# Row of the mLSTM decays: sent to all partitions by four DMAs instead of by products with a selecting row

## The chip, the cores and the metric

One Trainium2 chip, one of its NeuronCores. The metric is the device time of one execution in microseconds (us). The kernel before takes 950.82 us (median of three runs, 950.45 to 951.0).

## What is computed

One inference step of a hybrid streaming encoder with two layers. Two streams go through it together: a prompt of 256 new frames (T columns 0 to 255) and 64 sampled frames of a running stream (columns 256 to 319), so T = 320. A layer projects the normalised input into four head groups (a: convolution and linear recurrence, b: latent attention, c: retention, d: mLSTM), joins their outputs in an output projection, and ends in a SwiGLU network. All numbers are fp32. The change touches group d alone. Its step in the reference is:

```python
bh  = cumsum(lfc); igh = igc
dm  = where(tril, bh[..., :, None] - bh[..., None, :] + igh[..., None, :], -inf)
m_t = maximum(bh + m, max(dm, -1))
sc  = einsum('bthd,bshd->bhts', qc, kc) * exp(dm - m_t[..., None])
```

The kernel splits the exponent of one head h into a part that depends on the query t alone, `r2[h, t] = bh[t] - m[t]`, and a part that depends on the key s alone, `r1[h, s] = ig[s] - bh[s]`. Scores are kept with the keys on the partitions and the queries along the row. So r1 is a number per partition, and r2 is a row that all 128 partitions need.

## The kernel before, in words

Each engine has its own instruction stream, written out by hand in the order in which it runs (TensorE from line 694, ScalarE from 1262, VectorE from 1560, GpSimd from 586, the queue of weight loads from 502). They are tied by semaphores alone. The products of TensorE write eight banks of PSUM; `layer_uses` (129) gives each result its banks in order, `claim` makes TensorE wait until the previous user of a bank has been read, and `fill` signals that a result is there.

Weights stream through a ring of five slots; a slot is loaded again when its last product is done. Layers run one after the other. Within a layer the order on TensorE is: the input projections (`feature`, line 743: 16 instructions of 128x320 for an output of 128 rows), then stage d, stage b (attention), stage c (retention), the output projection (1068), and the SwiGLU products (1111), which take over half of the time.

Stage d is four heads long. TensorE runs `d_scores(0)`, and then for each head h: one projection for stage c (for h = 3 the key transposes of stage b and half a projection), `d_scores(h+1)` ahead of need, and `head_out(h)`, the value products. `d_scores(h)` is the three score products (771 to 773) and, for the decays, one product of the 4x128 table `headrow` with the 4x320 tile `r2` (928), which puts row h of r2 on all partitions, in bank 4 or 5 (`dd0` to `dd3`). VectorE then runs `decay_arg(h)`: three additions of a mask (1806) that read this bank and write `dmx`. ScalarE takes three exponentials of it (1415 to 1417) with r1 as the bias. VectorE multiplies the scores (1853) and the values (1801, the helper `tails`) by the result, which releases `head_out(h)` (`need(pe, "w_d", ...)`; its first product is line 781). VectorE's order is `decay_arg(0)`, and then for each h the multiplications of h, `decay_arg(h+1)`, after h = 0 the keys of stage b (`key_rows`, 1843 to 1846), and `d_out(h-1)` (1821 to 1834).

The row r2 is made by VectorE (1753) in 4 partitions, one for each head; 1756 is the last of that group of instructions and signals `m_rows`, on which GpSimd waits before it sends out the states `p_mm` and `s_mm` (recorded at line 615, the helper `out`). TensorE's products of stage d come some 21 us later.

`arena` is a scratch tile of 128 x 10624 numbers; `pr`, the attention probabilities, lies in it from `bstart + 1280`, and is first written in stage b. `latents_loaded` counts the loads of the attention's latents (three DMAs in each layer, 16 counts each).

Of the kernel before, what the change touches and what calls it, by code (L numbers as in the profile page):

```python
# [68 lines left out]
def constants():  # L69

    parts, at, n = [], {}, 0

    def put(name, a):
        nonlocal n
        full = np.zeros((P, a.shape[1]), np.float32)
        full[:a.shape[0]] = a
        at[name] = (n, a.shape[1])
        parts.append(full)
        n += a.shape[1]

    i = np.arange(P)
    put("ident", np.eye(P))
    put("ones", np.ones((P, P)))
    put("headmean", (i[:, None] // HD == i[None, :] // HD) / HD)
    put("swap", (i[:, None] == (i[None, :] ^ 32)))

    pos = np.concatenate([np.arange(SEQ), PAST + np.arange(DEC), np.zeros(TP - T)]).astype(np.float32)
    inv = (np.float32(10000.0) ** (-np.arange(16, dtype=np.float32) / np.float32(16))).astype(np.float32)
    ang = (pos[:, None] * inv[None, :]).astype(np.float32).reshape(NT, P, 16).transpose(1, 0, 2)
    put("cos_t", np.concatenate([np.cos(ang), np.cos(ang)], 2).reshape(P, NT * 32))  # L90
    put("sin_t", np.sin(ang).reshape(P, NT * 16))
    row_head = lambda pair: 2 * pair + i // HD
    put("headrow", np.repeat(np.eye(H), P, 1))
    put("pairrow", np.concatenate([(row_head(p)[None, :] == np.arange(H)[:, None]) for p in range(2)], 1))
    put("early", (i[None, :] < 64) * (i[:, None] == 0))
    put("late", np.where(i[:, None] == 0, NEG, 0.0) * np.ones((1, 64)))
    diff = np.full((P, 512), -1, np.int64)
    diff[:, 0:256] = np.arange(256)[None, :] - i[:, None]
    diff[:, 256:384] = np.arange(128)[None, :] - i[:, None]
    diff[:, 448:512] = np.arange(64)[None, :] - i[:, None]  # L100
    ok = diff >= 0
    put("negmask", np.where(ok, 0.0, NEG))
    lg = np.log(1.0 - 2.0 ** (-5.0 - np.arange(H)))
    put("decay", np.concatenate([np.where(ok, np.exp(np.where(ok, diff, 0) * lg[h]), 0.0) for h in range(H)], 1))
    put("cross", np.concatenate([np.exp((np.arange(DEC)[None, :] + 1.0) * lg[row_head(p)][:, None])
                                 for p in range(2)], 1))
    inv = (np.float32(10000.0) ** (-np.arange(32, dtype=np.float32) / np.float32(32))).astype(np.float32)
    ang = (pos[None, :T] * inv[i % 32][:, None]).astype(np.float32)
    put("cos_f", np.cos(ang))
    put("sin_f", np.sin(ang) * np.where(i % 64 < 32, -1.0, 1.0)[:, None])  # L110
    return np.concatenate(parts, 1).astype(np.float32), at
# [17 lines left out]
def layer_uses():  # L129
    u = [("cpT", (2,)), ("ms1", (3,))]  # L130
    u += [(f"kv{i}", (i + 1,)) for i in range(3, KTILES)]
    dense = [0]

    def d(*names):
        for n in names:
            u.append((n, (dense[0] % 2,)))
            dense[0] += 1

    d("ql0", "ql1", "kvr", "mo0", "mo1", "mig", "mfg", "mv0", "mv1")
    u += [("cnT", (4,)), ("qms", (5,))]  # L140
    d("mvt0", "mvt1")
    u += [("qt0", (6,)), ("qt1", (7,)), ("qt2", (2,))]
    d("mq0", "mq1", "mk0", "mk1")
    u += [(f"kv{i}", (4 + i,)) for i in range(3)]
    u += [("rT", (3,)), ("gx", (2,)), ("mkt", (6, 7))]
    for h in range(H):
        u += [(f"ds{h}", (2 + h % 2,)), (f"dd{h}", (4 + h % 2,)), (f"do{h}", (6 + h % 2,))]
    d("rq0", "rq1", "rk0", "rk1")
    fill = [("rv1",), ("rqs0", "lx0", "rqs1", "rvt0", "rvt1"), ("rks0", "lx1", "rks1"), ("rg0",)]
    u += [("bk0", (4, 5)), ("bq0", (6,))]  # L150
    d("rv0")
    u += [("bs0", (2, 3))]
    for h in range(H):
        if h == 1:
            u += [("dT", (0, 1))]
        if h + 1 < H:
            u += [(f"bk{h + 1}", (4, 5)), (f"bq{h + 1}", (6,))]
        d(*fill[h])
        u += [(f"bp{h}", (4, 5))]
        if h + 1 < H:  # L160
            u += [(f"bs{h + 1}", (2, 3))]
        else:
            u += [("ga0", (6,)), ("gx0_", (2,)), ("ga1", (3,))]
            d("gx1_", "rg1")
        u += [(f"bo{h}", (7,))]
    u += [("rkt", (4, 5)), ("bT", (6, 7))]
    for h in range(H):
        u += [(f"cs{h}", (2 + h % 2,)), (f"co{h}", (4 + h % 2,))]
    d("lg0", "lg1")
    u += [("am0", (6,)), ("am1", (7,)), ("cT", (6, 7))]  # L170
    u += [(f"o{n}", (n,)) for n in range(KT)]
    u += [("ms2", (2,)), ("fa0", (0,)), ("fb0", (1,))]
    for j in range(1, FT):
        u += [(f"fa{j}", (3 * (j % 2),)), (f"fb{j}", (3 * (j % 2) + 1,)), (f"fc{j}", (3 * (j % 2) + 2,))]
    for q in range(NQ):
        u += [(f"ya{q}", (3 * (q % 2),)), (f"yb{q}", (3 * (q % 2) + 1,)), (f"yc{q}", (3 * (q % 2) + 2,))]
    return u
# [25 lines left out]
def build(nc, I, O):  # L203
    with ExitStack() as ctx:
# [5 lines left out]
        def sem(name):  # L210
            if name not in sems:
                sems[name] = ctx.enter_context(nc.semaphore(name))
            return sems[name]
# [6 lines left out]
        def C(name, rows=P):  # L220
            a, n = cat[name]
            return cst[0:rows, a:a + n]
# [31 lines left out]
        def view(base, n, **kw):  # L254
            assert base + n <= AR, (base, n)
            return arena[:, base:base + n]
# [29 lines left out]
        qT = view(bstart + 896, TP)  # L286
        pr = view(bstart + 1280, 1024)
        pT = view(bstart + 2304, 1024)

        b = 0  # L290
        xpad = take(2 * 326).rearrange("p (k n) -> p k n", k=2)
# [99 lines left out]
        def claim(pe, use, l):  # L391

            for prev in before[use]:
                if prev is not None:
                    k = banks[prev][0]
                    pe.wait_ge(read[k], l * nfill[k] + order[prev])
                elif l > 0:
                    for k in {banks[last[b_]][0] for b_ in banks[use]}:
                        pe.wait_ge(read[k], l * nfill[k])
                else:  # L400
                    top = max(banks[use])
                    pe.wait_ge(sem("x_turned"), top + 1)
                    if 0 in banks[use]:
                        pe.wait_ge(sem("cols_ready"), 1)

        def bank(use, a, n, rows_=P):
            base = banks[use][0] * 512
            return flat[0:rows_, base + a:base + a + n]
# [4 lines left out]
        def need(eng, name, l, n, k=None):  # L413

            assert per.setdefault(name, n) == n, name
            eng.wait_ge(sem(name), l * n + (n if k is None else k))
# [16 lines left out]
        def now_read(eng, use):  # L433

            eng.sem_inc(read[banks[use][0]], 1)
# [151 lines left out]
        def _(pool):  # L587
# [25 lines left out]
            def out(dst, src):  # L613
                nout[0] += 1
                pool.dma_start(dst, src, allow_slow_non_contiguous=True).then_inc(sem("out_done"), 16)  # L615
# [12 lines left out]
            for l in range(DEPTH):  # L628
# [22 lines left out]
                out(O["p_krope"][l, 0].rearrange("(t p) c -> p t c", p=P), krr[:, 0:2, :])  # L651
                out(O["s_krope"][l, 0], krr[0:DEC, 2, :])
                need(pool, "m_rows", l, 1)
                out(O["p_mm"][l].rearrange("b h -> h b"), mro[:, SEQ - 1:SEQ])
                out(O["s_mm"][l].rearrange("b h -> h b"), mro[:, T - 1:T])
                pool.wait_ge(sem("out_done"), 16 * nout[0])
# [38 lines left out]
        def _(pe):  # L695
            mm = nc.tensor.matmul

            def fill(ins, use):
                ins.then_inc(filled[banks[use][0]], 1)
# [104 lines left out]

            def past_latents(l):
                claim(pe, "cpT", l)
                pe.wait_ge(sem("latents_loaded"), 48 * (l + 1))
                for a in range(4):
                    ins = nc.tensor.transpose(bank("cpT", a * P, P), pckv[:, a, :], ident)
                fill(ins, "cpT")  # L810

            for l in range(DEPTH):
# [109 lines left out]

                def d_scores(h):
                    causal_scores(f"ds{h}", l, h)
                    u = f"dd{h}"
                    claim(pe, u, l)
                    sel = C("headrow", H)[:, h * P:(h + 1) * P]
                    fill(mm(bank(u, 0, T), sel, r2[:, :], start=True, stop=True), u)  # L928

                def turn_keys(h, what="kq"):  # L930
                    if "k" in what:
# [629 lines left out]
        def _(dve):  # L1561
# [92 lines left out]
            for l in range(DEPTH):  # L1654
# [146 lines left out]
                    return v.tensor_tensor(vw[:, h % 2, :, 0:e], vaug[:, :, h, 0:e], end, ALU.mult)  # L1801

                def decay_arg(h):
                    wait_filled(dve, f"dd{h}", l)
                    for a, q0, n in ((0, 0, 256), (256, 128, 128), (448, 256, 64)):
                        step(v.tensor_tensor(dmx[:, a:a + n], bank(f"dd{h}", q0, n), C("negmask")[:, a:a + n], ALU.add),
                             "dmx" if a == 448 else None)
                    now_read(dve, f"dd{h}")

                def d_out(h):  # L1810

# [375 lines left out]
```

## Time and profile before

| | |
|---|---|
| median of three runs | 950.82 us |
| the profiled execution, its own time | 950.9 us |
| its span, first to last instruction | 949.1 us |
| TensorE busy (PE) | 939.3 us, 99% |
| VectorE (DVE), ScalarE (ACT), GpSimd (POOL) busy | 505.5, 203.7, 394.6 us |
| TensorE's granted clock | 1.0 (2.4 GHz) |
| moved by DMA | 112.12 MB, 118 GB/s on average |

PE is the matrix engine's products, PEld its weight loads, SP the queue that issues weight loads. Times in the profile are us from the start of the span. An fp32 product shows as two MATMUL instructions. POOL's DMA_DIRECT2D rows are GpSimd issuing a DMA in software; their duration is the issue alone and not the transfer.

### The profile page before, as it was taken

Reading aid. Unit: us, or ns where it says so; the run is one execution under the profiler, and the core shown is the slowest. Engines: PE = TensorE matmul, PEld = TensorE weight load, DVE = VectorE, ACT = ScalarE, POOL = GpSimd, SP = SyncE. Lnnn points to the kernel's source line nnn. Section 1 sums busy time; section 2 is a strip of 40 time slices with the busy share of each in tenths; the row PEclk is TensorE's granted clock in tenths of the full one; section 3 lists DMA queues with packets and bytes.
Section 4 is the critical chain, followed back from the end, with each engine's and each line's share of the span. In section 5 each row is a group of like instructions: output and inputs, shape, how many; then the busy total and the mean of one; then the engine's idle time right before and its main releaser. Section 6 shows DMA issues by size and latency. Waiting matters only on the chain.

```text
span 949.1 us, 14973 instructions
## 1 busy us (share of the span) xinstructions
PE 939.3 (99%) x5782; PEld 822.1 (87%) x5782; DVE 505.5 (53%) x1037; ACT 203.7 (21%) x445; POOL 394.6 (42%) x385
## 2 busy tenths in 40 slices
PE   8999999999999999999999999999999999999998
PEld 6776777877999999999977677777789999999998
DVE  5473656864555656512253555668346565653321
ACT  2223244433011000100031243454320000001001
POOL 6200200033976666676311003002159666666770
PEclk9999999999999999999999999999999999999999
DMA  9942211308555444343443312121375444444421
GB/s 280 234 134 90 89 47 46 93 8 217 145 148 146 135 134 135 122 153 126 120 129 112 106 61 76 35 75 50 65 195 140 134 134 133 136 136 136 139 87 47
DMA packets 159314, 112.12 MB, mean 118 GB/s; under 512 B 10118, under 2 KB 157228, under 8 KB 159116
## 3 DMA queue, kind: packets, MB, share of 16 engines
q1 hardware_dynamic: 154660, 104.50, 37.9%
q0 software_dynamic: 3952, 5.92, 2.4%
q8 instruction: 46, 0.75, 0.3%
q10 hardware_dynamic: 632, 0.75, 0.3%
q14 instruction: 24, 0.20, 0.1%
HBM read 108.89 MB, written 2.27 MB: 117 GB/s over the span
## 4 chain that ended last, share of the span: by engine, by line
PE 96%; DVE 1%; ACT 1%; ACTq 0%; issue 0%; POOL 0%; DVEq 0%; POOLq 0%
PE ps L1111 51%; PE ps L743 19%; PE ps L1068 7%; PE ps L1129 2%; PE ps L852 1%; PE ps L824 1%; PE ps L953 1%; PE ps L889 1%; PE ps L1007 1%; PE ps L1016 1%; PE ps L771 1%; PE ps L791 1%; PE ps L928 1%; PE ps L936 1%; PE ps L1049 0%; PE ps L781 0%
## 5 line engine op out<-in xcount | busy, mean ns | idle before, releaser
L743 PE MATMUL ps<-hT,ring 128*128 128x320 f32 x672 | 187.9, 435 | 2.2 <-DVE hT L1580 1.7
L743 PEld LDWEIGHTS ps<-hT,ring 128*128 128x128 f32 x672 | 124.9, 190 | 56.2 <-DVE hT L1580 3.9
L604 POOL TENSOR_TENSOR work<-ring 128x512 f32<-128x512 f32 (+1 forms) x66 | 81.7, 1238 | 155.2 <-issue 112.6
L1111 PE MATMUL ps<-mixT,ring 128*128 128x160 f32 x672 | 105.0, 299 | 0.0
L1111 PE MATMUL ps<-hT,work 128*128 128x160 f32 x672 | 98.5, 299 | 0.0
L1111 PE MATMUL ps<-hT,ring 128*128 128x160 f32 x672 | 98.1, 299 | 0.0
L1111 PEld LDWEIGHTS ps<-mixT,ring 128*128 128x128 f32 x672 | 95.9, 190 | 0.0
L1111 PEld LDWEIGHTS ps<-hT,ring 128*128 128x128 f32 x672 | 93.7, 190 | 0.3
L1111 PEld LDWEIGHTS ps<-hT,work 128*128 128x128 f32 x672 | 93.7, 190 | 0.0
L606 POOL TENSOR_TENSOR work<-ring 128x512 f32<-128x512 f32 (+1 forms) x66 | 82.2, 1246 | 5.2
L605 POOL TENSOR_TENSOR ring<-ring 128x512 f32<-128x512 f32 (+1 forms) x66 | 82.2, 1245 | 5.2
L607 POOL TENSOR_TENSOR work<-ring,work 128x512 f32<-128x512 f32 (+1 forms) x66 | 81.9, 1241 | 5.2
L1532 ACT ACTIVATE arena<-ps 128x160 f32<-128x160 f32 x42 | 12.7, 303 | 286.9 <-PE ps L1111 286.9
L1068 PE MATMUL ps<-mixT,ring 128*128 128x320 f32 x256 | 71.1, 435 | 0.0
L2120 DVE TENSOR_TENSOR arena<-arena,ps 128x160 f32<-128x160 f32 x8 | 2.6, 321 | 118.6 <-ACT arena L1550 118.6
L1068 PEld LDWEIGHTS ps<-mixT,ring 128*128 128x128 f32 x256 | 48.0, 190 | 19.2
L615 POOL DMA_DIRECT2D out_p_ret<-sst x8 | 4.2, 525 | 141.1 <-DVE sst L1978 141.1
L1111 PE MATMUL ps<-work,ring 128*128 128x160 f32 x352 | 55.7, 299 | 0.0
L1111 PE MATMUL ps<-mixT,work 128*128 128x160 f32 x336 | 52.5, 299 | 0.0
L1111 PE MATMUL ps<-arena,work 128*128 128x160 f32 x352 | 51.7, 299 | 0.0
L1111 PEld LDWEIGHTS ps<-work,ring 128*128 128x128 f32 x352 | 50.4, 190 | 0.0
L1111 PEld LDWEIGHTS ps<-arena,work 128*128 128x128 f32 x352 | 49.1, 190 | 0.0
(394 smaller groups left out, 1386.2 us busy)
## 6 DMA issues: line engine op xcount, KB each, us to landing
ring<-in_w_gu SPq DMA_DIRECT2D x88, 512.0 KB, 5.2
ring<-in_w_in SPq DMA_DIRECT2D x44, 512.0 KB, 4.8
ring<-in_w_down SPq DMA_DIRECT2D x32, 512.0 KB, 4.4
ring<-in_w_out SPq DMA_DIRECT2D x16, 512.0 KB, 4.4
ring<-in_w_down SPq DMA_DIRECT2D x16, 384.0 KB, 3.5
cst<-in_consts POOLq DMA_DIRECT2D x1, 1664.0 KB, 12.7
ring<-in_w_in SPq DMA_DIRECT2D x2, 640.0 KB, 5.3
wqb<-in_mla_wq_b POOLq DMA_DIRECT2D x2, 384.0 KB, 6.7
```

Of the source, the lines that this page charges most:

```text
L604: step(tt(s3, a11, a21, ALU.subtract))
L605: step(tt(a21, a21, a22, ALU.add))
L606: step(tt(s2, a21, a11, ALU.subtract))
L607: step(tt(s4, a12, s2, ALU.subtract), "mixed")
L743: ins = mm(bank(use, 0, T, m), w[:, k, c:c + m], hT[:, k, 0:T], start=(k == 0), stop=(k == KT - 1))
L771: mm(bank(use, 0, 256), k[:, 0:128], q[:, 0:256], start=True, stop=True)
L791: ins = mm(bank(use, 200 + 64 * s, 64, e), a, b_, start=(t == tiles[0]), stop=(t == tiles[-1]))
L824: fill(mm(bank(f"kv{i}", 0, 512), lat, wkvb[:, :], start=True, stop=True), f"kv{i}")
L1068: ins = mm(bank(u, 0, T), w[:, k, (n % 2) * P:(n % 2 + 1) * P], mixT[:, k, :], start=(k == 6), stop=(k == 5), skip_group_check=True)
L1111: ins = mm(bank(use, at * HT, HT), left, right(k), start=(opens and k == 0 and at == 0), stop=(closes and k == n - 1), skip_group_check=True)
L1129: return mm(bank(use, 0, T), w[:, k, q * P:(q + 1) * P], xg[:, k, :], start=(k == 0), stop=(k == KT - 1))
L1532: step(A(p1c[:, j % 2, :], bank(f"fa{j}", 0, HT), ACT.Copy), "p1_copied")
```

## The change

The four products with `headrow`, their bank uses and the table itself go. In their place GpSimd issues four DMAs after `m_rows`, ahead of the two state outputs. Each copies one row of r2 (320 numbers, 1280 bytes) from its one partition to all 128 partitions of a view `r2b[h]` in the arena. `decay_arg(h)` reads this view, after a wait for all four. The waits on the shared semaphore count 16 x 4 more in each layer.

```diff
-    put("headrow", np.repeat(np.eye(H), P, 1))
...
-        u += [(f"ds{h}", (2 + h % 2,)), (f"dd{h}", (4 + h % 2,)), (f"do{h}", (6 + h % 2,))]
+        u += [(f"ds{h}", (2 + h % 2,)), (f"do{h}", (6 + h % 2,))]
...
+        r2b = [view(bstart + (1280 + h * T if h < 3 else 2560), T) for h in range(H)]
...
                 need(pool, "m_rows", l, 1)
+                for h in range(H):
+                    pool.dma_start(r2b[h], r2[h:h + 1, :].unsqueeze(1).broadcast_to([1, P, T])).then_inc(sem("latents_loaded"), 16)
...
-                pe.wait_ge(sem("latents_loaded"), 48 * (l + 1))
+                pe.wait_ge(sem("latents_loaded"), 48 + (48 + 16 * H) * l)
...
                 def d_scores(h):
                     causal_scores(f"ds{h}", l, h)
-                    u = f"dd{h}"
-                    claim(pe, u, l)
-                    sel = C("headrow", H)[:, h * P:(h + 1) * P]
-                    fill(mm(bank(u, 0, T), sel, r2[:, :], start=True, stop=True), u)
...
                 def decay_arg(h):
-                    wait_filled(dve, f"dd{h}", l)
+                    dve.wait_ge(sem("latents_loaded"), (48 + 16 * H) * (l + 1))
                     for a, q0, n in ((0, 0, 256), (256, 128, 128), (448, 256, 64)):
-                        step(v.tensor_tensor(dmx[:, a:a + n], bank(f"dd{h}", q0, n), C("negmask")[:, a:a + n], ALU.add),
+                        step(v.tensor_tensor(dmx[:, a:a + n], r2b[h][:, q0:q0 + n], C("negmask")[:, a:a + n], ALU.add),
                              "dmx" if a == 448 else None)
-                    now_read(dve, f"dd{h}")
```

## Rows read from the trace of the kernel before

**Rows 1.** The page: busy us by engine, and the chain that ended last
```profile
PE 939.3 (99%) x5782; PEld 822.1 (87%) x5782; DVE 505.5 (53%) x1037; ACT 203.7 (21%) x445; POOL 394.6 (42%) x385
...
PE 96%; DVE 1%; ACT 1%; ACTq 0%; issue 0%; POOL 0%; DVEq 0%; POOLq 0%
```
**Rows 2.** Waits of TensorE: total us, times, longest; largest and first of stage b
```profile
PE ps L743 <- DVE hT L1580: 1.7, 1, 1.7
...
PE ps L978 <- DVEq L435: 0.8, 2, 0.4
```
**Rows 3.** The product with the selecting row, by its line
```profile
L928 PE MATMUL ps<-r,cst x16: 427/480/532, 87.6 to 573.4; 4*128 4x320 f32 x16
...
  DVE work L1806: 16.6, 8
```
**Rows 4.** Timeline of TensorE, layer 0, stage d: start us, us
```profile
87.36 0.33 PE L773 MATMUL ps<-work 128*128 128x64 f32 x2
87.62 0.80 PE L928 MATMUL ps<-r,cst 4*128 4x320 f32 x2
88.36 4.58 PE L743 MATMUL ps<-hT,ring 128*128 128x320 f32 x16
...
93.42 0.33 PE L773 MATMUL ps<-work 128*128 128x64 f32 x2
94.41 0.43 PE L781 MATMUL ps<-work 128*128 128x65 f32 x2
94.69 0.39 PE L782 MATMUL ps<-work 128*128 128x65 f32 x2
94.91 0.39 PE L783 MATMUL ps<-work 128*128 128x65 f32 x2
```
**Rows 5.** Timeline of TensorE, layer 1, stage c: scores without a selecting product
```profile
635.38 0.33 PE L773 MATMUL ps<-work 128*128 128x64 f32 x2
635.55 4.53 PE L743 MATMUL ps<-hT,ring 128*128 128x320 f32 x16
```
**Rows 6.** Timeline, layer 0: from the row r2 to the weights of head 0
```profile
64.22 0.48 DVE L1753 TENSOR_TENSOR r<-work,mro 4x320 f32<-4x320 f32 x1
65.87 0.54 POOL L615 DMA_DIRECT2D out_p_mm<-mro  x1 [15.05 <-DVE nm L1756]
86.45 0.62 DVE L1793 TENSOR_TENSOR work<-work,glb 128x128 f32<-128x128 f32 x2 [2.89 <-ACT glb L1399]
88.56 1.01 DVE L1806 TENSOR_TENSOR work<-ps,cst 128x256 f32<-128x256 f32 x3 [1.50 <-PE ps L928]
91.92 0.36 DVE L1801 TENSOR_TENSOR work<-work 128x195 f32<-128x195 f32 x1
```
**Rows 7.** Timeline, layer 1: VectorE and TensorE around head 3
```profile
577.80 0.36 DVE L1801 TENSOR_TENSOR work<-work 128x195 f32<-128x195 f32 x1
578.31 0.41 PE L781 MATMUL ps<-work 128*128 128x65 f32 x2
```
**Rows 8.** A broadcast load: its issue on GpSimd, and KB and us to landing
```profile
17.58 0.75 POOL L643 DMA_DIRECT2D bcn<-in_mla_kv_norm  x1
...
bcn<-in_mla_kv_norm POOLq DMA_DIRECT2D x1, 128.0 KB, 7.5
```
**Rows 9.** Stretches: PE, PEld, DVE, ACT, POOL busy, PEclk, DMA share, GB/s
```profile
22.00:23.00 1.00, 1.00 (x5) 0.75 (x4) 0.00 (x0) 0.00 (x0) 1.00 (x3) 1.00 1.03 400
...
66.00:70.00 4.00, 4.00 (x17) 2.82 (x16) 2.68 (x6) 0.83 (x3) 0.91 (x2) 1.00 0.01 0
70.00:75.00 5.00, 5.00 (x20) 3.58 (x19) 4.44 (x9) 0.44 (x1) 0.00 (x0) 1.00 0.68 210
```
**Rows 10.** GpSimd's software queue, and a wait for a small output's end
```profile
q0 software_dynamic: 3952, 5.92, 2.4%
...
POOL out_p_mC L615 <- DMA out_s_mn<-sst: 6.6, 4, 1.6
```
**Rows 11.** Timeline, layer 1, stage c: the last VectorE wait on projections; an addition in SBUF
```profile
631.42 0.49 DVE L1914 TENSOR_SCALAR work<-ps 128x320 f32<-128x320 f32 x1 [3.27 <-PE ps L743]
...
665.17 0.43 DVE L2040 TENSOR_TENSOR mixT<-arena 128x256 f32<-128x256 f32 x1
```
**Rows 12.** Timeline, layer 0: the weight loads behind the row r2
```profile
69.37 24.51 SPq L554 DMA_DIRECT2D ring<-in_w_in  x6
```

## The prediction

> **What bounds the kernel now.** I read the page first. TensorE's products are busy 939.3 of 949.1 us, and the chain that ended last lies on it for 96% [rows 1]. Its table of waits has 1.7 us as its largest entry, in layer 0 before stage d, and 0.8 us in two layers at the head of stage b [rows 2]. So every microsecond of TensorE's stream counts, as long as its inputs are there, and the other engines matter only where they would be late. The reader is to see two things in the rows by line and in the timeline: how long TensorE really spends on a selecting product, and how much time lies between the moment the row r2 exists and the moment its copy is needed. The first is the gain, the second is what the new transfer may take for nothing.
>
> **What goes on TensorE.** Line 928 has 16 instructions, two for each of 8 products, with a median of 480 ns [rows 3]. They overlap, so I take starts instead of durations. In stage d the last score product starts at 87.36 and the projection behind the selecting product at 88.36, 1.00 us later [rows 4]. Stage c has the same scores with no selecting product behind them, and the projection follows after 0.17 us (635.38 to 635.55) [rows 5]. The difference is 0.83 us. At head 1 the value product follows the scores by 0.99 us (93.42 to 94.41), and the next one is 0.28 us behind it, where the one after that has 0.22 (94.69 to 94.91) [rows 4]. With the 0.17 to 0.22 us of an undisturbed step this too gives 0.8 to 0.85. Eight products are 8 x 0.83 = 6.6 us. On this alone 950.9 becomes 944.3.
>
> **What is moved on VectorE and ScalarE.** The additions read SBUF instead of PSUM. An addition of 128x256 with all of its operands in SBUF takes 0.43 us [rows 11], and the three additions of a head, of 256, 128 and 64 columns, take 1.01 us from PSUM [rows 6]. If all three cost as much as the widest it would be 1.3 us, 0.3 more, in the shadow of waits that go; if they scale, it is the same. I cost it at 0. VectorE waited 16.6 us for the eight products [rows 3], and these waits go. For heads 1 to 3 that makes the decays early: at head 3 the weights were ready at 577.80 + 0.36 = 578.16 and TensorE came at 578.31 [rows 7], a margin of 0.15. TensorE would now come 4 x 0.83 = 3.3 us earlier, and this margin would be gone if VectorE kept its times. It does not: its additions for head 3 no longer wait for a product late in the stage, only for their turn. What is late next is the scores of head 3, which come from TensorE itself. Behind stage d the last long wait of VectorE in stage c is on a projection (3.27 us at 631.42) [rows 11], so the group work behind it moves with TensorE. I take the whole 3.3 us of each layer as kept.
>
> **What is moved on GpSimd and in the start.** Four issues stand ahead of the two state outputs. A broadcast load took 0.75 us to issue [rows 8], so these outputs leave 3 us later; VectorE asks for them only in stage c, whose rows lie past 631 in layer 1 [rows 11], when stage d was over at 580 [rows 7]. Cost 0, and nothing would come of 3 us more. Without `headrow` the constants are 512 columns (256 KB) fewer in the first 30 us. None of TensorE's larger waits names that load; 0, with at most a few tenths to gain.
>
> **What is added: the transfer.** This decides. GpSimd can issue from 65.87 on [rows 6]. VectorE would be free for the first additions at 86.45 + 0.62 = 87.07. From their start to the end of head 0's weights it was 91.92 + 0.36 - 88.56 = 3.72 us [rows 6]. TensorE will come to `head_out(0)` two products earlier than 94.41 [rows 4], at 92.75. So the four copies must have landed by 92.75 - 3.72 = 89.03, which is 23.2 us after the first issue. Each us beyond it is a us of waiting on TensorE, once in a layer: after that wait the decays of the next heads are made while a projection of 4.5 us runs, and don't stop it again. Layer 1 has the same distances.
>
> No row shows a DMA that reads one partition of SBUF many times, so I bound it. The low end is the nearest by form: a broadcast of 128 KB that landed 7.5 us after its issue, beside full queues [rows 8]. Four issues of 0.75 us behind each other make 7.5 + 2.3, about 10 us. But its source was memory, not SBUF. The high end is from the source. All 4 x 128 x 1280 B = 655 KB come out of four neighbouring partitions of SBUF, the same 5 KB again and again. If they serve one DMA engine at a time, all sixteen engines together get the pace of one. The most that sixteen showed is 400 GB/s [rows 9], 25 GB/s for one, and 655 KB take 26.2 us. With the first issue (0.75) and 1.6 us from the last issue to the end of a small output [rows 10] the last copy is there after 28.6 us. That is 5.4 us too late, in each of two layers 10.8 us. A third number is further out: the software queue's packets took 2.4% of 16 x 949.1 us for 3952, 92 ns each [rows 10]; one at a time 512 packets take 47 us.
>
> I take the middle one, 28.6 us. What speaks for it is that the destination is spread and the source is not, and that a row which many read has one place to be read from. It costs 10.8 - 6.6 = 4.2 us: **955.1 us** against the profiled execution's 950.9; against the median of 950.82 the same sum gives 955.0. That is my forecast.
>
> The Trainium skill bears on exactly this term: the page "SBUF — State Buffer", section "Door 1: The DMA port swizzle", says that a DMA's rate goes by how many of sixteen ports its partitions reach, and puts partitions 0 to 3 on one port with an asymptote of about 27 GB/s. By that figure the estimate for the 655 KB is 24 us and the landing 26.5 us after the first issue, the wait 3.3 us a layer, and the sum 950.9. The page's own measurement is a transfer over four partitions, and no run here shows it yet for reading.
>
> The weight loads share the engines. Their next one goes out at 69.37 [rows 12]; the DMA share was 0.01 just before and 0.68 just after, at 210 GB/s [rows 9]. These are for slots used in stage b, tens of us later. I cost their delay at 0; if the cover were gone TensorE would show a wait for the ring.
>
> **Rivals.**
> (1) The copies land in time. The engines have room between 62 and 87 us [rows 9], a broadcast of nearly the same size took 7.5 us [rows 8], and 10 us is far under 23.2. Against it stands only the one source. Then nothing waits and the result is 950.9 - 6.6 = 944.3. It decides from a landing under 23.2 us, and it is faster while the landing stays under 25.5 us.
> (2) Packets are served one at a time, with their whole latency, as slowly as those of the software queue: 0.75 + 47 + 1.6 = 49.5 us, 26.3 us too late in each layer, 944.3 + 52.6 = 997. For it speaks the mean of 92 ns [rows 10]; against it that this mean holds many small packets with memory behind them.
> (3) The copies land in time but TensorE's earlier arrival is given back, because stage b or c was already as tight as head 3 was (0.15 us) [rows 7]: about 950. Against it: VectorE's long waits there are on TensorE.
>
> **How the numbers follow.** The forecast's mechanism, a landing set by the one source and a wait at head 0, has 0.57. Its time is 944.3 + 2 x (landing - 23.2): from 950 by a quicker source to 960 at 31 us, which is its own range. Rival 1 has 0.32, rival 2 0.06, rival 3 0.05. A measurement of this kernel tells a change from none at about 0.2%, 1.9 us. Of the forecast's 0.57 I give 0.14 to landings of 25.5 to 27.4 us, within that band. Faster is rival 1 and a little of rival 3, 0.34; the same 0.17; slower 0.49. The range goes from 943.2, under rival 1, to 960; rival 2 and longer landings are left out.
>
> **What the profile will show.** No instructions on line 928, and 0.17 to 0.22 us from the last score product to what follows. Four GpSimd issues of about 0.75 us behind `m_rows`. In the timeline, VectorE's first additions of each layer start late, at about 94.5 us where 87.1 was possible, with the transfer as what ended the wait; TensorE waits some 5.4 us at line 781, once in each layer, and nowhere else in the stage. If the first additions start at 87.1, rival 1 holds and the forecast is wrong in its largest term. If TensorE waits there and at more heads too, the wait is not paid once. If VectorE's additions became slower than 1.01 us a head, reading SBUF was not free.

## The result, and the profile after

The changed kernel takes 953.9 us (median of seven runs, 952.2 to 954.36), the kernel before on the same chip 950.63 us (seven runs, 950.45 to 951.0). The ratio is 1.0029, with a 95% interval of 1.0018 to 1.0041: slower by 3.3 us. The profiled execution took 953.82 us, its span is 952.0.

The page of the changed kernel, with its line of TensorE, the chain that ended last by engine and by line, and the software queue (packets, MB, share of 16 engines):

```profile
PE 936.7 (98%) x5766; PEld 822.8 (86%) x5766; DVE 505.5 (53%) x1037; ACT 203.8 (21%) x445; POOL 399.2 (42%) x393
...
q0 software_dynamic: 4272, 6.97, 6.9%
...
PE 90%; DMA 5%; DVE 3%; ACT 1%; issue 1%; POOL 0%; DVEq 0%; ACTq 0%; POOLq 0%
PE ps L1109 51%; PE ps L745 14%; PE ps L1066 7%; DMA arena<-r 5%; PE ps L1127 2%; PE ps L854 1%; PE ps L951 1%; PE ps L891 1%; PE ps L793 1%; PE ps L1005 1%; PE ps L1014 1%; PE ps L706 1%; PE ps L773 1%; PE ps L934 1%; PE ps L1047 0%
```

The reader sees three things. TensorE has the 16 instructions fewer, and still the span is longer. The copy of the row now has 5% of the chain that ended last; no DMA stood in it before [rows 1]. And the software queue has 320 packets more, but its share of the DMA engines went from 2.4% [rows 10] to 6.9%: these few packets are slow.

TensorE's waits (total us, times, longest). The first line is new; the second stood at the top before [rows 2]:

```profile
PE ps L783 <- DVE work L1799: 5.5, 2, 2.8
PE ps L745 <- DVE hT L1578: 1.7, 1, 1.7
```

Line 783 is the first value product of a head (781 before). It waits once in each layer, at head 0. VectorE and GpSimd in layer 0, which answer to [rows 6]:

```profile
65.59 2.18 POOL L655 DMA_DIRECT2D arena<-r  x4 [15.07 <-DVE nm L1754]
67.75 0.53 POOL L615 DMA_DIRECT2D out_p_mm<-mro  x1
...
91.46 1.01 DVE L1804 TENSOR_TENSOR work<-arena,cst 128x256 f32<-128x256 f32 x3 [4.69 <-DMA arena<-r]
...
94.88 0.36 DVE L1799 TENSOR_TENSOR work<-work 128x195 f32<-128x195 f32 x1
```

TensorE there, which answers to [rows 4]:

```profile
87.07 0.33 PE L775 MATMUL ps<-work 128*128 128x64 f32 x2
87.24 4.53 PE L745 MATMUL ps<-hT,ring 128*128 128x320 f32 x16
91.60 0.59 PE L773 MATMUL ps<-work 128*128 128x256 f32 x2
...
92.26 0.33 PE L775 MATMUL ps<-work 128*128 128x64 f32 x2
95.39 0.66 PE L783 MATMUL ps<-work 128*128 128x65 f32 x2 [2.80 <-DVE work L1799]
95.85 0.63 PE L784 MATMUL ps<-work 128*128 128x65 f32 x2
...
98.21 6.34 PE L745 MATMUL ps<-hT,ring 128*128 128x320 f32 x16
```

The selecting product is gone: 0.17 us from the last score product to the projection, where it was 1.00. The additions wait 4.69 us for the copies and start at 91.46, 25.87 us after the first issue. TensorE then waits 2.80 us. And behind that wait everything on TensorE is slower: a value product of 65 columns takes 0.63 us where it had 0.39, and the projection behind the head 6.34 us where the same one had 4.53 just before. The stretches say why (us, PE, PEld, DVE, ACT, POOL busy, PEclk, DMA share, GB/s):

```profile
70.00:75.00 5.00, 5.00 (x20) 3.57 (x19) 4.15 (x9) 0.44 (x1) 0.00 (x0) 1.00 0.78 23
75.00:80.00 5.00, 5.00 (x16) 2.66 (x14) 0.50 (x2) 1.59 (x4) 0.00 (x0) 1.00 1.13 34
80.00:85.00 5.00, 5.00 (x27) 3.74 (x27) 2.03 (x5) 3.74 (x7) 0.00 (x0) 1.00 0.96 32
...
90.00:95.00 5.00, 2.59 (x13) 1.93 (x11) 1.84 (x6) 1.25 (x3) 0.00 (x0) 1.00 0.96 324
...
95.00:96.00 1.00, 0.61 (x3) 0.64 (x4) 0.93 (x3) 0.00 (x0) 0.00 (x0) 0.52 1.10 347
96.00:97.00 1.00, 1.00 (x7) 1.00 (x6) 0.86 (x5) 0.58 (x2) 0.00 (x0) 0.50 1.10 349
...
101.00:102.00 1.00, 1.00 (x4) 0.69 (x3) 0.81 (x3) 0.00 (x0) 0.00 (x0) 0.57 0.00 0
102.00:103.00 1.00, 1.00 (x5) 0.73 (x4) 0.84 (x5) 0.39 (x1) 0.00 (x0) 1.00 0.00 0
```

The granted clock is 0.50 (1.2 GHz, the lower of its two levels) for some 6.8 us in layer 0; it falls at 95.0, shortly before the wait ends at 95.39. In layer 1 it falls 0.7 us behind the end of the wait (562.00) and stays low for some 3.4 us:

```profile
562.00:563.00 1.00, 0.99 (x8) 1.00 (x8) 0.90 (x4) 0.00 (x0) 0.00 (x0) 0.83 1.10 347
563.00:564.00 1.00, 1.00 (x8) 1.00 (x8) 0.86 (x5) 0.94 (x3) 0.00 (x0) 0.50 1.10 347
...
566.00:567.00 1.00, 1.00 (x5) 0.76 (x4) 0.96 (x2) 0.00 (x0) 0.00 (x0) 0.96 0.13 47
```

The last two columns of the stretches show another thing. While the copies run, from 70 to 90, the DMA engines are busy (share 0.78 to 1.13 of all sixteen) and yet move 23 to 34 GB/s in all. Before, the same 20 us had 210 GB/s from 70 to 75 [rows 9], 28, then 185, and nothing from 85 on, 106 GB/s on average; of these stretches the third is

```profile
80.00:85.00 5.00, 5.00 (x27) 3.53 (x26) 2.29 (x6) 3.60 (x7) 0.00 (x0) 1.00 0.54 185
```

It isn't a single engine that does the copying, since the share is of all sixteen. The weight loads all but stop, and make up for it from 90 on at 324 to 349 GB/s. The copies by their line (ns of one issue, min, median, max, then us to landing):

```profile
L655 POOL DMA_DIRECT2D arena<-r x8: 537/540/583, 65.6 to 533.9; - x8
...
DMA to landing us min/median/max: 8.0/17.1/24.1
```

and the weight loads in the table of DMA issues (number, KB each, median us to landing), 4.8 us before:

```profile
ring<-in_w_in SPq DMA_DIRECT2D x44, 512.0 KB, 6.5
```

The four copies land one after the other, the first after 8.0 us, the last after 24.1. The first lands at 65.59 + 8.0 = 73.59 and the last at 91.46, so on the mean one takes (91.46 - 73.59) / 3 = 5.96 us for its 163.8 KB: 27.5 GB/s.

### The profile page after: what moved, and what is told of

Read it like the earlier page. It is cut to its first block, busy times and chain, and to the rows that moved or that the text cites. A ratio compares the mean times of both kernels' runs of the same rounds, so it can differ in the third digit from the quotient of the medians.

```text
span 952.0 us, 14945 instructions
## 1 busy us (share of the span) xinstructions
PE 936.7 (98%) x5766; PEld 822.8 (86%) x5766; DVE 505.5 (53%) x1037; ACT 203.8 (21%) x445; POOL 399.2 (42%) x393
## 4 chain that ended last, share of the span: by engine, by line
PE 90%; DMA 5%; DVE 3%; ACT 1%; issue 1%; POOL 0%; DVEq 0%; ACTq 0%; POOLq 0%
PE ps L1109 51%; PE ps L745 14%; PE ps L1066 7%; DMA arena<-r 5%; PE ps L1127 2%; PE ps L854 1%; PE ps L951 1%; PE ps L891 1%; PE ps L793 1%; PE ps L1005 1%; PE ps L1014 1%; PE ps L706 1%; PE ps L773 1%; PE ps L934 1%; PE ps L1047 0%
## 5 line engine op out<-in xcount | busy, mean ns | idle before, releaser
L745 PE MATMUL ps<-hT,ring 128*128 128x320 f32 x672 | 190.6, 440 | 2.2 <-DVE hT L1578 1.7
## 6 DMA issues: line engine op xcount, KB each, us to landing
arena<-r POOLq DMA_DIRECT2D x8, 160.0 KB, 17.1
```

Of the source, the lines that this page charges most:

```text
L745: ins = mm(bank(use, 0, T, m), w[:, k, c:c + m], hT[:, k, 0:T], start=(k == 0), stop=(k == KT - 1))
```

## The experiments

The question is what the 3.3 us are made of. My theory: the products' removal is kept in full; the copies' one source makes them late; their lateness costs TensorE twice, as a wait and as a stretch at half clock. The rivals: the copies' mere presence costs (held-back weights, issues on GpSimd); the software queue is what is slow; the clock falls by itself. Runs of one group shared their runs of the kernel before (medians 950.66, 950.56, 950.71 and 950.54 us).

**One copy instead of four.**

```diff
-                for h in range(H):
+                for h in range(1):
...
-                        step(v.tensor_tensor(dmx[:, a:a + n], r2b[h][:, q0:q0 + n], ...
+                        step(v.tensor_tensor(dmx[:, a:a + n], r2b[0][:, q0:q0 + n], ...
```

> Edit: only row 0 is copied, and the decays of all four heads are computed from it, so heads 1 to 3 work with a wrong row. Theory (the 655 KB leave SBUF at the pace of one engine because their source is one place; TensorE waits 2.8 us at head 0 of each layer and then runs part of its stream at half clock): a quarter of the bytes lands some 8 us after the issue, the first additions start at about 86.8 us, TensorE waits nowhere in stage d, its clock stays at 1.0, and the whole 6.6 us of the removed products show: 944.0 us. Rival (reading SBUF, the extra issues or delayed weight loads cost the time, not the landing): part of the cost stays, over 947 us.

This kernel leaves out the rows of heads 1 to 3, whose decays are made from that of head 0. 943.15 us (942.99 to 944.9, four runs), ratio 0.9918 (0.9905 to 0.9932). The copy landed after 7.6 us and no wait is left at head 0. So the loss comes with the later copies, and without it the change would be worth 7.5 us.

**Head 0 waits for its own copy alone.** All four copies stay; the first counts on a semaphore of its own.

```diff
-... .then_inc(sem("latents_loaded"), 16)
+... .then_inc(sem("latents_loaded" if h else "row0"), 16)
...
-                    dve.wait_ge(sem("latents_loaded"), (48 + 16 * H) * (l + 1))
+                    if h == 0:
+                        dve.wait_ge(sem("row0"), 16 * (l + 1))
+                    else:
+                        dve.wait_ge(sem("latents_loaded"), (48 + 16 * (H - 1)) * (l + 1))
```

> Edit: all four copies as in the changed kernel, but head 0 waits on a semaphore of its own for its own copy, heads 1 to 3 for the other three. Theory: the copies are served in order, some 6 us each; head 0's lands 8 us after its issue, the rest at 91.3 us, when VectorE has head 0's weights ready (90.5) and TensorE needs those of head 1 only at about 99. No wait of TensorE in stage d, clock 1.0, 944.0 us, with the copies taking as long as before (last landing 25.8 us after the first issue). Rival (the copies cost time by holding back the weight loads): over 947 us. Rival (the four copies share the engines and finish together, near 25 us): 953.9 us, no gain.

943.13 us (943.01 to 943.97, five runs), ratio 0.9917 (0.9903 to 0.993), with a clock of 1.000 over the whole span. The timeline of layer 0, VectorE's additions of heads 0 and 1, then TensorE:

```profile
86.77 1.01 DVE L1807 TENSOR_TENSOR work<-arena,cst 128x256 f32<-128x256 f32 x3
...
91.34 1.01 DVE L1807 TENSOR_TENSOR work<-arena,cst 128x256 f32<-128x256 f32 x3 [0.54 <-DMA arena<-r]
...
92.22 0.33 PE L775 MATMUL ps<-work 128*128 128x64 f32 x2
92.39 0.39 PE L783 MATMUL ps<-work 128*128 128x65 f32 x2
92.61 0.39 PE L784 MATMUL ps<-work 128*128 128x65 f32 x2
```

and two of its stretches:

```profile
70.00:75.00 5.00, 5.00 (x20) 3.54 (x19) 4.12 (x9) 0.44 (x1) 0.00 (x0) 1.00 0.74 22
...
90.00:95.00 5.00, 5.00 (x34) 4.16 (x33) 3.93 (x14) 1.70 (x4) 0.00 (x0) 1.00 0.98 331
```

The copies are as slow as in the changed kernel (median 17.1 us to landing, 22 GB/s in all from 70 to 75), and head 1's additions still come 0.54 us late for them. Yet TensorE doesn't wait for them, since these have a projection's 4.5 us of room. The whole loss hung on head 0 waiting for three copies that it doesn't need. Slow copies, held-back weights and four issues cost nothing by themselves. Head 0's copy, now with a semaphore of its own, landed 8.1 us after its issue.

This run also gives the accounting. From GpSimd's first action on the rows to the first of the long score products of stage b, the kernel before took 53.48 us in layer 0 and 53.46 in layer 1, this one 49.71 in both, the changed kernel 55.84 and 54.30. So the removal is worth 3.77 + 3.75 = 7.5 us, and the changed kernel loses 6.13 + 4.59 = 10.7 us to this one. Its waits are 2.80 + 2.75 = 5.5 us; the other 5.2 fit the low clock: behind the ends of the waits TensorE worked at half clock for some 9.9 us, and half of that is 5.0.

**Work in the place of the wait.** Five products that nobody uses, of 128x320, just ahead of `head_out(0)`.

```diff
+                        claim(pe, "dm", l)
+                        for _ in range(5):
+                            ins = mm(bank("dm", 0, T), C("ones"), hT[:, 0, 0:T], start=True, stop=True)
+                        fill(ins, "dm")
...
```

> Edit: in the changed kernel TensorE runs five idle products of 128x320 (2.7 us) just ahead of its wait at head 0, into a bank that nobody uses then. Their result is used by nobody. Theory: the wait for the weights of head 0 ends as late as before, but TensorE is busy for nearly all of it; its granted clock stays at 1.0, and the 4.7 us that the stretch at half clock cost (3.1 in layer 0, 1.6 in layer 1) come back: 949.2 us. Rival (the clock fell for another reason, or the stretch behind the wait is slow because of the memory traffic): clock 0.5 again after the wait, 953.9 us.

949.04 us (948.91 to 950.64, ten runs), ratio 0.9983 (0.9974 to 0.9992): 4.9 us faster than the changed kernel, by more work. TensorE's timeline, in an execution in which all lies 1.6 us later from the start on (its clock had a mean of 0.84 from 10 to 20, where the changed kernel's had 1.00):

```profile
94.04 2.91 PE L969 MATMUL ps<-hT,cst 128*128 128x320 f32 x10
97.02 0.41 PE L784 MATMUL ps<-work 128*128 128x65 f32 x2
```

and the stretch behind it:

```profile
95.00:100.00 5.00, 4.93 (x30) 3.66 (x29) 3.89 (x14) 2.12 (x6) 0.00 (x0) 1.00 1.10 350
```

The head is late by the same copies (97.02, which less the 1.6 us is 95.4, for 95.39), but the clock stays at 1.00, in layer 1 too, with the same rush of weights (350 GB/s). So the low clock follows TensorE's idle time, not the DMA traffic, and costs about 5 us of its own.

**Another source.** The four copies read a table of 128 partitions, each its own.

```diff
-                    pool.dma_start(r2b[h], r2[h:h + 1, :].unsqueeze(1).broadcast_to([1, P, T])) ...
+                    pool.dma_start(r2b[h], C("cos_f")) ...
```

> Edit: the four copies take their 4 x 160 KB from a table of 128 partitions (each partition its own row) instead of from one partition; the numbers that the decays are made of are wrong. Same queue, bytes, packets, destination and waits. Theory (the source is the limit): landing within 10 us of the first issue, first additions at about 86.8 us, no wait of TensorE, 944.0 us. Rival (the software queue, the packets or the bytes set the pace): last landing still about 25 us after the first issue and 953.9 us.

This kernel leaves out the copying of r2. 943.17 us (942.95 to 943.4, four runs), ratio 0.9915 (0.9901 to 0.9928). The copies landed after 2.3 us (median) instead of 17.1, at the same size, queue and destination. The source alone makes them slow.

**The copies beside the kernel before.** They are made and never read, and their end is asked for ahead of stage b.

```diff
+                for h in range(H):
+                    pool.dma_start(r2b[h], r2[h:h + 1, :].unsqueeze(1).broadcast_to([1, P, T])).then_inc(sem("rows_copied"), 16)
...
+                    if h == 0:
+                        act.wait_ge(sem("rows_copied"), 16 * H * (l + 1))
```

> Edit: the kernel before with its products and its additions from PSUM as they were, and the four copies beside them; nothing reads the copies, and only the exponentials of stage b wait for them. Theory (the copies cost through the wait at head 0 alone): the weight loads are held back for the some 20 us in which the copies run, but no weight is late; 950.7 us, unchanged, no new wait of TensorE. Rival (the copies cost by what they take from the other transfers): TensorE waits for a weight or an input and the time is over 951.5 us.

950.86 us (950.47 to 952.39, ten runs), ratio 1.0004 (0.9995 to 1.0014): no difference. The transfers of others are held back just the same, as the stretch from 70 to 75 shows (210 GB/s without the copies):

```profile
70.00:75.00 5.00, 5.00 (x20) 3.51 (x19) 3.77 (x7) 0.00 (x0) 0.61 (x2) 1.00 0.96 28
```

and the landing of the weight loads issued from 60 to 100:

```profile
DMA to landing us min/median/max: 6.3/15.2/26.0
```

Without the copies the same loads took at most 5.3 us, so one was delayed by some 21 us, and that is hidden here; the first rival is out.

**By way of memory.** r2 is written to memory (5 KB) and the four broadcasts read it there.

```diff
...
+                pool.dma_start(rmem[l], r2[:, :]).then_inc(sem("rows_in_memory"), 16)
+                pool.wait_ge(sem("rows_in_memory"), 16 * (l + 1))
...
+                    pool.dma_start(r2b[h], rmem[l, h].partition_broadcast(P)).then_inc(sem("latents_loaded"), 16)
```

> Edit: the changed kernel, but the four rows are first written to memory (5 KB), and the four broadcasts read them from there; one wait for all four, as in the changed kernel. Theory (the slow part is reading one place of SBUF, not the broadcast): the write adds some 2 us and the issues 2.2 us, the broadcasts land as quickly as other loads, all within 12 us of the first issue; first additions at 86.7 us, no wait of TensorE, 943.1 us as with head 0 waiting alone. Rival (a broadcast, one source read 128 times, is slow from anywhere): landing over 23 us and 950 us or more.

943.05 us (942.94 to 944.81, five runs), ratio 0.9923 (0.9911 to 0.9936). Its DMA issues (KB each, median us to landing):

```profile
arena<-rmem POOLq DMA_DIRECT2D x8, 160.0 KB, 3.9
...
rmem<-r POOLq DMA_DIRECT2D x2, 5.0 KB, 1.6
```

and the stretch that had 23 GB/s:

```profile
70.00:75.00 5.00, 5.00 (x20) 3.51 (x19) 4.09 (x9) 0.44 (x1) 0.66 (x2) 1.00 0.93 262
```

The same repeated read is no trouble from memory: 3.9 us, and the weight loads land as quickly as in the kernel before (median 4.8 us in both).

**The hardware queue of ScalarE.** It issues the copies instead of GpSimd.

```diff
+                need(act, "m_rows", l, 1)
+                for h in range(H):
+                    act.dma_start(r2b[h], r2[h:h + 1, :].unsqueeze(1).broadcast_to([1, P, T])).then_inc(sem("rows_copied"), 16)
...
```

> Edit: the same four copies as in the changed kernel, issued by ScalarE on its hardware queue instead of by GpSimd in software, at about the same moment, with a semaphore of their own. Theory (the source sets the pace): the last copy lands some 25 us after the first issue as before, TensorE waits some 2.8 us at head 0 in each layer and runs at half clock behind it: 953 to 954 us. Rival (GpSimd's software queue with its packets is what is slow): landing within 10 us, no wait, 943.1 us.

952.29 us (948.99 to 954.21, ten runs), ratio 1.0012 (1.0 to 1.0024). The issue in the timeline:

```profile
65.56 9.71 ACTq L1378 DMA_DIRECT2D arena<-r  x4
```

the landing in the table of DMA issues:

```profile
arena<-r ACTq DMA_DIRECT2D x8, 160.0 KB, 16.7
```

TensorE's waits:

```profile
PE ps L781 <- DVE work L1800: 4.0, 2, 2.0
...
PE ps L771 <- ACTq L435: 1.1, 2, 0.6
```

and the stretches behind the wait of layer 0 (it ends at 95.62) and behind that of layer 1 (559.07):

```profile
95.00:100.00 5.00, 4.38 (x27) 3.62 (x28) 4.51 (x12) 1.69 (x4) 0.00 (x0) 1.00 0.48 166
...
560.00:565.00 5.00, 5.00 (x23) 3.97 (x23) 4.54 (x11) 1.70 (x4) 0.00 (x0) 0.71 0.27 88
```

The last copy landed 26.1 us after the first issue (91.70 less 65.56), as late as in the changed kernel, so the software queue isn't the reason. The four issues held ScalarE for 9.71 us, which made the first scores late as well. That left a wait of 2.0 us a layer instead of 2.8, and the time came out under the 953 to 954 expected. Behind the wait of layer 0 the clock stayed at 1.00, behind that of layer 1 it had a mean of 0.71. That is where the wide spread of these ten runs comes from as far as the runs show: their mean clock goes with their times, 1.000 in the run of 948.99 us, 0.998 in those of 950.7 to 950.9, 0.996 in those of 952.3 to 952.7 and 0.995 in those of 954.1 to 954.2. Why it falls after one wait of 2.0 us and not after another is open. One thing did differ with the queue: from 75 to 90 the DMA engines moved 74, 56 and 171 GB/s, for the 34, 32 and 27 of the changed kernel, so the other transfers were held back less beside the same copies.

**Partition or port.** Four source rows at once, each for 32 partitions, from three choices of partitions; these kernels leave out the copying of r2.

```diff
+                    pool.dma_start(r2b[h], C("cos_f")[0:4, :].unsqueeze(1).broadcast_to([4, 32, T])) ...
```

The other two read `[0:16:4, :]` and `[0:P:32, :]`.

> Leaves out the copying of r2: each of the four copies takes rows 0, 1, 2 and 3 of the cosine table, each sent to 32 partitions, so the decays' numbers are other ones; sizes, queue, place and destination are those of the changed kernel. Theory A, the limit is one port that neighbouring partitions share (the rule of the Trainium skill, page SBUF - State Buffer, Door 1): as slow as the changed kernel, the median landing near 17 us, the last near 24 us, a wait of about 2.8 us at head_out(0), about 954 us. Theory B, the limit is the single partition: four partitions serve four times as fast, 655 KB in about 6 us, median landing 4 to 7 us, no wait, about 943 us.

> As the run before it (the decays' numbers are other ones), but the four source rows are partitions 0, 4, 8 and 12 of the table. Theory A, by the port table of the same page these lie on four ports: four times the pace, 655 KB in about 6 us, median landing 4 to 7 us, no wait at head_out(0), about 943 us. Theory B, the single partition is the limit: the same numbers, so this run alone does not tell them apart; beside the run with partitions 0 to 3 it does. A third, that any copy inside SBUF with repeated reads is slow: median landing near 17 us, about 954 us.

> As the run before it (the decays' numbers are other ones), with source partitions 0, 32, 64 and 96. Theory A, by the page's table these lie on two ports (0 and 32 on one, 64 and 96 on the other): twice the pace of the changed kernel, 655 KB in about 12 us, median landing about 8 to 10 us, no wait at head_out(0) as the last lands some 14 us after the first issue, about 943 us. Theory B, the single partition is the limit: as with partitions 0, 4, 8 and 12, median landing 4 to 7 us.

Landing of the copies, min, median and longest, and the software queue (packets, MB, share of 16 engines), from partitions 0 to 3:

```profile
DMA to landing us min/median/max: 2.7/25.2/26.9
...
q0 software_dynamic: 5040, 6.98, 6.9%
```

from 0, 32, 64 and 96:

```profile
DMA to landing us min/median/max: 2.7/12.8/13.8
...
q0 software_dynamic: 5040, 6.98, 4.5%
```

and from 0, 4, 8 and 12:

```profile
DMA to landing us min/median/max: 2.9/7.0/7.9
...
q0 software_dynamic: 5040, 6.98, 3.4%
```

Only the longest of the three numbers is sound here. The four copies count on one semaphore, and counts of a later copy can stand in for the first one's: with partitions 0 to 3 a first copy of 163.8 KB landed in 2.7 us would be 60 GB/s, when the engines moved 19 GB/s in all from 65 to 70. From the first issue to the last landing it was 27.9, 15.9 and 10.0 us in layer 0. These are not one, two and four times the pace as they stand, but with some 4 us that all three spend besides (an estimate from these numbers) the rest is 24, 12 and 6 us. The shares of the engines' time say the same: over the 2.4% of the kernel before [rows 10] they are 4.5, 2.1 and 1.0 points, for the same bytes and packets. The Trainium skill, page "SBUF — State Buffer", section "Door 1: The DMA port swizzle", puts 0 to 3 on one port, the second set on two and the third on four; this is its order. The number of source partitions is four in each, and their distance (1, 32 and 4) doesn't order the three. So the limit is the port that four neighbouring rows share, not the row. The times are 959.83 (two runs), 943.12 (two) and 943.66 us (two), ratios 1.0096 (1.0067 to 1.0125), 0.992 (0.9892 to 0.9949) and 0.9926 (0.9897 to 0.9955).

My expectation for the first, 954 us, missed: the last copy landed at 93.57 instead of 91.46 in layer 0, 27.9 us after the first issue for 25.87, and 29.1 us after it in layer 1. This made TensorE wait 10.9 us in all, and around the end of each wait the clock was low for 6.8 us. That explains the sum: 943.1 + 10.9 + 5.8 for the clock. Why the 655 KB took 2 to 3 us longer in this form is open.

The versions in which head 0 waits for its own copy (943.13 us) and in which the row goes by way of memory (943.05 us) beat both kernels, by 7.5 us.

## Why the prediction was right, and where its sizes were off

The forecast was 955.0 us and its own range 950 to 960; 953.9 was measured. Its mechanism, a landing set by the one source and a wait at head 0 that is longer than the gain, is the one that the runs show. But its terms were off and one was missing, and that the number is so near is luck: where it has 10.8 us of waits, the runs have 5.5 us of waits and 5.2 of low clock.

- **What goes on TensorE: 6.6 us forecast, 7.5 measured.** I took 0.83 us for each product from the one ahead of a projection. Ahead of a value product it is 1.27 - 0.39 = 0.88 us over two steps (93.42 to 94.69 in [rows 4] against 92.22 to 92.61 with head 0 alone): the second step was slowed too, which I had seen as 0.28 against 0.22 and not summed. That makes 0.83 + 3 x 0.88 = 3.5 a layer; the value products of head 3 came some 0.1 us sooner behind the work ahead of them as well, and the rest of the 3.77 I haven't traced.
- **The landing: 28.6 us forecast, 25.87 measured.** The reason given, one source that serves at one pace whoever reads, is shown by the spread table and by the three sets of partitions. The pace was 27.5 GB/s for my 25. The figure of about 27 GB/s in the Trainium skill, page "SBUF — State Buffer", section "Door 1: The DMA port swizzle", was the nearer, and the landing of 26.5 us that I estimated from it too.
- **The wait at head 0: 5.4 us a layer forecast, 2.80 and 2.75 measured**, the difference almost all from the landing; the deadline of 89.03 was right within 0.4 us (91.46 - 2.80 = 88.66). That it comes once in each layer and nowhere else is what the list of waits shows.
- **Missing: the clock.** Nothing in the prediction gave a price to what TensorE does after a wait. It was 5.2 us, as much as the waits. With 7.5 and 5.5 us and no clock I would have said 949, slightly faster, and been wrong in sign. The changed kernel without its clock term is about what the filler gives, 949.04.
- **Costs put at nothing** held: additions from SBUF 1.01 us a head as from PSUM; issues (0.54 us each, not 0.75) and late state outputs without effect; weight loads held back without effect (950.86 with the copies beside). The stretch begins 0.28 us earlier than before (65.59 for 65.87), within the few tenths allowed for the smaller table.
- **Rivals.** Copies in time was not what happened, but it is what the variants reach: 943.1, where I had 944.3. Packets one by one, with 47 us, is out, and its count was wrong: beside the kernel before, the copies add 384 packets in the two layers (4336 on the software queue for 3952 [rows 10]), which is 192 a layer and not 512. That the gain is given back is out: 7.5 us were kept.

One choice of the reading I would make otherwise: the deadline was worked out for all four copies, since the diff waits for all four. The first alone is due then. Seen in the landing times (8.0 us the first, one more each 5.96 on the mean), that one wait, with the low clock behind it, is the whole difference between -7.5 and +3.3 us.

## What to carry to other kernels

A row that all partitions need is sent quickly by DMA from memory or from sources spread over the ports, and slowly (27.5 GB/s) from one place in SBUF, on both of the queues tried here; write it to memory first, or let each consumer wait for its own piece alone. Where TensorE bounds a kernel, look at the granted clock behind each wait in 1 us stretches: here waits of 2.8 us cost about twice their length, those of 4.9 and 6.0 us in the run with source rows 0 to 3 about half as much again, and of two waits of 2.0 us one cost nothing more. A slow copy on the software queue also takes the DMA engines from all others: ask what loads are due within its whole length.

## What the runs showed of the hardware beyond the expected

- While 655 KB were read from one port of SBUF, the other transfers nearly stopped: 23 to 34 GB/s in all for 20 us, of which the copies are 27.5, against 106 on average before. With the copies on ScalarE's queue they went on in part (56 to 171 GB/s in all from 75 to 90). It cost nothing here since no held-back load was due in that time.
- With an idle time of 2.80 us on TensorE came some 6.8 us at a clock of 0.50, with one of 2.75 us some 3.4 us, with those of 4.9 and 6.0 us (source rows 0 to 3) 6.8 us each, and of two of 2.0 us (ScalarE's queue) one was followed by some 3.4 us and the other by none.
- The four copies took 2.18 us to issue on GpSimd's software queue and 9.71 us on ScalarE's hardware queue. There the first two took 0.6 us each, as on GpSimd, and the others 3.8 and 4.6 us; no run shows what held them.
- A product of 4 rows (4x128 weights, 320 columns) costs 0.83 to 0.88 us on TensorE's stream, more than one of 128 rows with as many columns, which costs 0.55 (eight in the 4.36 us from 87.24 to 91.60).
